# Keys of the recurrent levels written by ScalarE as exponentials of sums, in place of a product on GpSimd

## The reference

```python
def forget(z, lb):
    f = lbh + (1.0 - lbh) * jax.nn.sigmoid(z)
    return 1.0 - f, jnp.log(f)          # key, log of the forget gate
...
cum = jnp.cumsum(lc, axis=2)
rel = cum[:, :, :, None, :] - cum[:, :, None, :, :]
decay = jnp.exp(jnp.where(lower_tri, rel, -jnp.inf))
scores = jnp.einsum('bhtk,bhtsk,bhsk->bhts', qc, decay, kc)
```

## Time and profile before

| | |
|---|---|
| median of 3 runs | 1273.4 us (1273.05 to 1275.78) |
| profiled execution | 1273.12 us |
| its span, first to last instruction | 1271.3 us |
| TensorE busy | 1239.5 us, 98% |
| VectorE busy | 861.2 us, 68% |
| ScalarE busy | 656.2 us, 52% |
| GpSimd busy | 97.3 us, 8% |
| mean granted TensorE clock | 0.996 |

### The profile page before, as it was taken

One profiled execution on the slowest core, in us unless ns is written; L12 is line 12 of the kernel. 1 busy time (PEld: TensorE's weight loads), 2 busy tenths in 40 slices (PEclk: granted clock), 3 DMA queues, 4 the chain that ended last, 5 costly groups with the idle time before them and its releaser, 6 DMA issues.

```text
span 1271.3 us, 22052 instructions
## 1 busy us (share of the span) xinstructions
PE 1239.5 (98%) x9208; PEld 1157.3 (91%) x9208; DVE 861.2 (68%) x1186; ACT 656.2 (52%) x1057; POOL 97.3 (8%) x152
## 2 busy tenths in 40 slices
PE   8999999999999999999999999999999999999998
PEld 7988989988888989989999998889899999999987
DVE  6897677654466677898666554657578987655543
ACT  5896665543368454452544443556563433544432
POOL 2100100000000000550100000000003520000000
PEclk9999999999998999999999999999999999999999
DMA  9542535555525323433555555433343325455552
GB/s 371 211 166 103 197 133 199 195 193 188 188 104 194 127 106 133 140 127 105 197 197 199 190 204 187 167 148 133 103 164 132 134 100 180 157 197 196 199 199 99
DMA packets 30323, 211.77 MB, mean 167 GB/s; under 512 B 3344, under 2 KB 3728, under 8 KB 5264
## 3 DMA queue, kind: packets, MB, share of 16 engines
q1 hardware_dynamic: 29936, 210.22, 46.1%
q10 hardware_dynamic: 288, 0.14, 0.0%
HBM read 209.29 MB, written 1.05 MB: 165 GB/s over the span
## 4 chain that ended last, share of the span: by engine, by line
PE 76%; DVE 12%; ACT 6%; issue 5%; DMA 0%; DVEq 0%; ACTq 0%
PE bank L534 74%; DVE w_lo L1651 3%; ACT w_hi L1152 2%; ACT W L1152 2%; DVE W L1632 1%; PE bank L634 1%; PE bank L869 1%; DVE W L1619 1%; DVE W L1618 1%; DVE xs L2154 1%; DVE W L2132 1%; DVE junk L2152 1%; DVE W L1642 1%; DVE x_lo L1662 0%; DVE stat L1591 0%
## 5 line engine op out<-in xcount | busy, mean ns | idle before, releaser
L1651 DVE TENSOR_TENSOR w_lo<-ring,w_hi 128x2048 fp32r<-128x2048 f32 x183 | 422.2, 2307 | 270.2 <-ACT w_hi L1152 269.8
L1152 ACT ACTIVATE w_hi<-ring 128x1024 fp32r<-128x1024 f32 (+1 forms) x368 | 366.3, 1047 | 223.1 <-PE bank L534 215.2
L534 PE MATMUL bank<-x_hi,w_lo 128*128 128x256 f32 x1840 | 253.8, 277 | 8.6 <-DVE w_lo L1651 7.6
L534 PE MATMUL bank<-x_hi,w_hi 128*128 128x256 f32 x1840 | 259.9, 280 | 2.2 <-ACT w_hi L1152 2.2
L534 PE MATMUL bank<-x_lo,w_hi 128*128 128x256 f32 x1840 | 246.9, 276 | 0.0
L534 PEld LDWEIGHTS bank<-x_hi,w_lo 128*128 128x128 f32 x1840 | 229.2, 188 | 11.4 <-DVE w_lo L1651 10.0
L534 PEld LDWEIGHTS bank<-x_hi,w_hi 128*128 128x128 f32 x1840 | 230.6, 188 | 5.8 <-issue 2.0
L534 PEld LDWEIGHTS bank<-x_lo,w_hi 128*128 128x128 f32 x1840 | 226.5, 188 | 0.0
L534 PE MATMUL bank<-W 128*128 128x128 f32 (+4 forms) x716 | 111.7, 329 | 8.5 <-ACT W L1152 4.8
L534 PEld LDWEIGHTS bank<-W 128*128 128x128 f32 (+3 forms) x716 | 88.0, 188 | 21.6 <-issue 12.5
L534 PE MATMUL bank<-w_hi,hid_hi 128*128 128x512 f32 x304 | 76.6, 389 | 0.0
(11 more groups left out here) (255 smaller groups left out, 1217.3 us busy)
## 6 DMA issues: line engine op xcount, KB each, us to landing
ring<-weight_pieces SPq DMA_DIRECT2D x191, 1024.0 KB, 4.8
const<-constants SPq DMA_DIRECT2D x1, 1376.5 KB, 10.1
W<-x_features SPq DMA_DIRECT2D x4, 256.0 KB, 5.2
ring<-weight_pieces SPq DMA_DIRECT2D x2, 512.0 KB, 6.1
h<-x SPq DMA_DIRECT2D x2, 512.0 KB, 11.9
W<-rg_weights SPq DMA_DIRECT2D x1, 1024.0 KB, 10.5
xs<-mem_features SPq DMA_DIRECT2D x1, 1024.0 KB, 11.3
oT<-mem SPq DMA_DIRECT2D x1, 1024.0 KB, 12.5
```

What stands on the lines that cost most here:

```text
L534: return nc.tensor.matmul(out, lhsT, rhs, start=first, stop=last)
L1152: return nc.scalar.activation(out, in_, ACT.Copy, scale=scale)
L1651: v.tensor_tensor(whole(w_lo, q), rows, whole(w_hi, q).bitcast(F32), ALU.subtract).then_inc(s_weight_low, 1)
```

## The change

The keys' logarithm is taken once in each layer. A new step `keyfloor`, placed in VectorE's list alone, writes the keys with a floor under them into `A_LK`; ScalarE takes their `Ln` right behind that of `F`. After the last scan VectorE makes two versions of the shifted sums: `F`, which now has the logarithm added in the backward half, and `FK`, with the logarithm subtracted in the forward half; that is 4 instructions instead of 2. `level_decay` reads `FK` for its first half, so that the key halves of `A_X` hold the logarithm of decay times key. ScalarE then takes four exponentials of 64x256 for each level and pair: two in place for the queries' decays, and two from `A_X` into `A_KL` for the keys. GpSimd only clears `A_KL`.

```diff
+A_LK = A_GATE + 3072
+A_FK = A_X + 2048
@@ the list of steps
-b[0], ("high", c[0][-1]), ("forget", l, 1), ("low", c[0][-1]), ("high", c[1][-1]), b[1], ...
+b[0], ("high", c[0][-1]), ("forget", l, 1), ("low", c[0][-1]), dve(("keyfloor", l)), ("high", c[1][-1]), b[1], ...
@@ gpsimd, decay
-                    if hp == 0:
-                        if idx:
-                            pool.wait_ge(s_key, idx)
-                        for both_hp in range(2):
...
-                            link(nc.gpsimd.memset(at(A_KL + 512 * ((idx + both_hp) % 4), 2 * S), 0.0))
...
-                    link(nc.gpsimd.tensor_tensor(kl[0:64, :, 0, :], kk[0:64, :, 0, :], x[0:64, :, 0, :], ALU.mult))
-                    nc.gpsimd.tensor_tensor(kl[64:128, :, 1, :], kk[64:128, :, 1, :], x[64:128, :, 1, :], ALU.mult).then_inc(s_key, 1)
+                    if idx >= 4:
+                        prev = idx - 4
+                        wait_filled(pool, f"level{prev // (2 * len(LEVELS))}.{prev // 2 % len(LEVELS)}{prev % 2}")
+                    nc.gpsimd.memset(at(A_KL + 512 * (idx % 4), 2 * S), 0.0).then_inc(s_cleared, 1)
@@ scalar, forget
+                        act.wait_ge(s_key_floor, l + 1)
+                        nc.scalar.activation(at(A_LK, 4 * S), at(A_LK, 4 * S), ACT.Ln).then_inc(s_log_k, 1)
@@ scalar, decay
-                    x = at(A_X + 512 * (idx % 4), 512)
-                    nc.scalar.activation(x, x, ACT.Exp).then_inc(s_decay, 1)
+                    x, kl = (at(a + 512 * (idx % 4), 2 * S).rearrange("p (b w c) -> p b w c", w=2, c=LEVELS[i]) for a in (A_X, A_KL))
+                    nc.scalar.activation(x[0:64, :, 1, :], x[0:64, :, 1, :], ACT.Exp)
+                    nc.scalar.activation(x[64:128, :, 0, :], x[64:128, :, 0, :], ACT.Exp).then_inc(s_decay, 1)
+                    act.wait_ge(s_cleared, idx + 1)
+                    nc.scalar.activation(kl[0:64, :, 0, :], x[0:64, :, 0, :], ACT.Exp)
+                    nc.scalar.activation(kl[64:128, :, 1, :], x[64:128, :, 1, :], ACT.Exp).then_inc(s_key, 1)
@@ vector, level_decay
-                v.tensor_tensor(x[:, :, :, 0, :], mid, f5[:, :, :, 0, :], ALU.subtract)
+                v.tensor_tensor(x[:, :, :, 0, :], mid, fk[:, :, :, 0, :], ALU.subtract)
@@ vector, keyfloor
+                    dve.wait_ge(s_hgrn_k, l + 1)
+                    v.tensor_scalar(at(A_LK, 4 * S), at(A_KK, 4 * S), 2.0 ** -63, None, ALU.max).then_inc(s_key_floor, 1)
@@ vector, after the last scan
+                        dve.wait_ge(s_log_k, l + 1)
                         v.tensor_copy(F[0:64, :, :], E[0:64, :, 1:S + 1])
-                        link(v.tensor_copy(F[64:128, :, :], E[64:128, :, 0:S]))
+                        v.tensor_tensor(F[64:128, :, :], E[64:128, :, 0:S], LK[64:128, :, :], ALU.add)
+                        v.tensor_tensor(FK[0:64, :, :], E[0:64, :, 1:S + 1], LK[0:64, :, :], ALU.subtract)
+                        link(v.tensor_copy(FK[64:128, :, :], E[64:128, :, 0:S]))
```

More of the change, by code:

```diff
@@ L138 @@
 A_KR = 0
+A_LK = A_GATE + 3072
+A_FK = A_X + 2048
 ARENA = A_QKT + 2048
-assert A_X + 2048 <= ARENA and A_SC1 + 6 * 512 <= ARENA
+assert A_FK + 1024 <= ARENA and A_SC1 + 6 * 512 <= ARENA
 def attention_plan():
@@ L276, in build @@
         s_bound_in, s_bound_exp, s_bounds, s_f, s_log_f, s_hgrn_k = (sem(n) for n in ("lb_in", "lb_exp", "lb_ready", "f_ready", "log_f_ready", "hgrn_k_ready"))
+        s_key_floor, s_log_k, s_cleared = sem("key_floor"), sem("log_key_ready"), sem("level_keys_cleared")
         s_decay_log, s_decay, s_query, s_key = (sem(n) for n in ("decay_log", "decay", "level_queries", "level_keys"))
@@ L429, in build @@
             steps += [kr, ("high", b[0][-1]), ("lora", l), ("low", b[0][-1]), ("znorm", l, 0), f1, ("high", b[1][-1]), ("low", b[1][-1]), ("forget", l, 0), ("znorm", l, 1)]
-            steps += [b[0], ("high", c[0][-1]), ("forget", l, 1), ("low", c[0][-1]), ("high", c[1][-1]), b[1], ("zturn", l), ("bsquare", l), c[0], ("low", c[1][-1])]
+            steps += [b[0], ("high", c[0][-1]), ("forget", l, 1), ("low", c[0][-1]), dve(("keyfloor", l)), ("high", c[1][-1]), b[1], ("zturn", l), ("bsquare", l), c[0], ("low", c[1][-1])]
             attend([(f"mla{l}", n) for n in range(4)] + [(f"diff{l}", n) for n in range(4)],
@@ L1615, in level_decay @@
                 x = at(A_X + 512 * (idx % 4), 2 * S).rearrange("p (g b w c) -> p g b w c", g=2, w=2, c=half)
-                f5 = F[:, 2 * hp:2 * hp + 2, :].rearrange("p g (b w c) -> p g b w c", w=2, c=half)
+                fk, f5 = (f[:, 2 * hp:2 * hp + 2, :].rearrange("p g (b w c) -> p g b w c", w=2, c=half) for f in (at(A_FK, 4, S), F))
                 mid = E[:, 2 * hp:2 * hp + 2, half:S:2 * half][:, :, :, None].broadcast_to([P, 2, nb, half])
-                v.tensor_tensor(x[:, :, :, 0, :], mid, f5[:, :, :, 0, :], ALU.subtract)
+                v.tensor_tensor(x[:, :, :, 0, :], mid, fk[:, :, :, 0, :], ALU.subtract)
                 v.tensor_tensor(x[:, :, :, 1, :], f5[:, :, :, 1, :], mid, ALU.subtract).then_inc(s_decay_log, 1)
@@ L1939, in _ @@
                     v.tensor_scalar(F, F, 2.0 ** -63, None, ALU.max).then_inc(s_f, 1)
+                elif kind == "keyfloor":
+                    l = step[1]
+                    dve.wait_ge(s_hgrn_k, l + 1)
+                    v.tensor_scalar(at(A_LK, 4 * S), at(A_KK, 4 * S), 2.0 ** -63, None, ALU.max).then_inc(s_key_floor, 1)
                 elif kind == "bnorm":
@@ L1962, in _ @@
                     if hd == 3:
+                        FK, LK = at(A_FK, 4, S), at(A_LK, 4, S)
+                        dve.wait_ge(s_log_k, l + 1)
                         v.tensor_copy(F[0:64, :, :], E[0:64, :, 1:S + 1])
-                        link(v.tensor_copy(F[64:128, :, :], E[64:128, :, 0:S]))
+                        v.tensor_tensor(F[64:128, :, :], E[64:128, :, 0:S], LK[64:128, :, :], ALU.add)
+                        v.tensor_tensor(FK[0:64, :, :], E[0:64, :, 1:S + 1], LK[0:64, :, :], ALU.subtract)
+                        link(v.tensor_copy(FK[64:128, :, :], E[64:128, :, 0:S]))
                 elif kind == "znorm":
```

9 lines of the change are left out of this document (removed).

## The result

The changed kernel takes 1291.8 us (median of 4 runs, 1291.1 to 1294.1). The kernel before took 1273.5 beside it (4 runs, 1273.05 to 1275.8). The ratio is 1.0146, with a 95% interval from 1.0133 to 1.0158. So it is slower by 18.3 us. The prediction had the sign right and the size wrong by a factor of three, with the time above the end of its range: +5.9 us expected, 1279.3, range to 1287.0. The profiled execution of the changed kernel has a span of 1290.0 us, against 1271.3 before.

The account below looks back on a forecast made before the run. VectorE was taken to bound turns 2 to 5, ScalarE's path turns 0 and 1. Turns with relief +0.95, second `Ln` +0.96 and sums +1.19 make 3.10 us a layer, 6.2 in both: 1279.3 us, range 1274.5 to 1287.

Parts of the forecast that it names:

- The new cycle: Turns, first decay to the next turn's: 8.19 us after the change, 9.14 with the copies in turns 0 and 1.
- The step that failed: Turns, ScalarE: eight 64x256 exponentials priced by a 128x256 row at 0.32 us each, 2.56 us in all.
- The upper bound: Turns: if exponentials do not overlap, eight take 3.36 us, each turn 0.80 more, +9.6 us.
- This rival: Turns: exponentials do not overlap or are slower at narrow strides, 1288.9 us; chance 0.15, shared with blocking clears.
- clears that block VectorE: Turns: GpSimd's clears block VectorE as multiplications do, turns above 9 us, up to 1292 us; chance 0.15, shared.
- the estimate of 2.45 us for eight: Turns: exponentials priced from the Trainium skill at 0.306 us each, giving a total 1.3 us below the forecast.
- The relief ahead of turn 0: VectorE ahead of turn 0: a sum no longer runs beside a GpSimd multiplication, -0.53 us a layer.
- The `Ln`: Second `Ln` on ScalarE, ahead of `w_hi` and four copies TensorE waits for: +0.96 us a layer.
- The sums: Behind the last scan: two added 64x1024 VectorE instructions, 2.30 us, delay `w_lo` and TensorE: +1.19 us a layer.
- the three signs of being wrong: Profile after: eight exponentials at 3 us or more, turns at 7.5, or TensorE's busy time changing beyond the clock term.
- TensorE does not become the limit: Turns: TensorE's own work, taken as 7.5 us a turn, stays below the new cycle.
- The faster rival: Turns: exponentials leave the cycle and TensorE sets the turn at 7.5 us, 1267.3 us; chance 0.05.

Follow-up runs that it names:

- the control with the moved `w_hi`: The kernel before with `w_hi` issued ahead of the decays in turns 0 to 5: 1271.47 us, ratio 0.9971.
- The run on all partitions: The changed kernel with each of its four exponentials over 128 partitions instead of 64, keys first: 1279.98 us, ratio 1.0062.
- one reordered step: The changed kernel with `w_hi` issued ahead of the decays in turns 0 to 5: 1269.22 us, ratio 0.9956.
- two smaller moves: Changed kernel with `w_hi` first, second `Ln` behind the head sums' square, two sums behind the gate drain after the last scan: 1263.0 us, ratio 0.991.

## Why the prediction was wrong

**The bound.** That turns 2 to 5 were bound by VectorE and turns 0 and 1 by ScalarE's path was right. The kernel with GpSimd's multiplications left out and the control with the moved `w_hi` show it from both sides.

**The new cycle.** Right in its parts and in its order: 0.78, `w_hi` 2.04, `w_lo` 2.21, drain 0.60 as taken, and VectorE's wait ahead of `w_lo`, released by ScalarE, at 2.20 to 2.27 us in turns 2 to 5 (1.5 to 2.5 foreseen; 3.3 in turns 0 and 1). The run on all partitions has the predicted cycle to 0.1 us (8.09 for 8.19).

**The step that failed** is "The nearest row is one of 128x256, which lasts 0.42 us and lets the next start after 0.32". The duration held (0.42). The overlap of 0.10 did not, because each exponential of the change works on the other half than the one before it. The term was 2.56 us and measured 3.49 (3.67 in turns 4 and 5, where the narrow halves add 0.18), so 0.93 to 1.11 more a turn. Over 12 turns that is 8 x 0.93 + 4 x 1.11 = 11.9 us of the 12.5 by which the median missed. The upper bound was named, "each costs its whole 0.42, 3.36 in all", and even it was 0.13 short: 0.02 lie between an exponential's end and the next one's start. This rival shared a chance of 0.15 with clears that block VectorE, and its time was 1288.9. The blocking clears' "up to 1292" is nearer in number, but they didn't come: `w_lo` took 2.29 us. The range went only two thirds of the way to 1288.9.

**A row that was there to be read.** The argument against that rival was that `w_hi` overlaps the activations ahead of it. All those run over all 128 partitions. The timeline of before has a pair of ScalarE in a row on opposite halves, copies from the lower to the upper half and back:

```profile
432.39 1.27 ACT L1152 ACTIVATE W<-W 64x512 f32<-64x512 f32 x2 [3.66 <-DVE W L1858]
433.57 0.57 ACT L1152 ACTIVATE xs<-bank 128x512 f32<-128x512 f32 x1
```

Two instructions of 64x512 take 1.27 us, 0.63 each, so they don't overlap. The copy behind them, on all partitions, then overlaps the second, which reads the upper half and writes the lower, by 0.09. So it seems to be the partitions written that count. The copies were not looked for because they aren't exponentials.

**The Trainium skill.** "ScalarE: Activation LUTs", "What ACT_TABLE_LOAD costs", says that back-to-back activations overlap by about 93 ns. The trace agrees where the first partition stays the same (0.40 to 0.42 long, step 0.31 to 0.33) and not for changing halves (step 0.43 to 0.44). The measurement decides, and the estimate of 2.45 us for eight was 1.04 too low.

**The remaining terms.** The relief ahead of turn 0 was right (-0.57 for -0.53), as was that clears don't disturb VectorE: in these turns they run beside its idle time, and in the run without multiplications `w_lo` takes 2.29 us with both clears (2 x 0.52) inside it. `keyfloor` (0.69 us at 400.34) delayed nothing. The `Ln` cost its 0.95 at its place, and half of that was given back in the first layer, where the low-clock stretch turned out shorter. The sums cost 1.41 for 1.19. Copies to `w_hi` took 1.11 instead of 0.95 in turns 0 and 1, 0.6 us in all. They take 0.95 in the run on all partitions, so it goes with the half-partition exponentials ahead of them; how is open. Two queries span 1.5 us instead of 1.28, since the second waits for ScalarE; each lasts 0.69, and nothing hangs on it. Two of the three signs of being wrong came true, the eight at over 3 us and TensorE's busy time, 6.7 us up, which is stretched by its waits.

**"TensorE does not become the limit"** held, and its limit, put at 7.5, is 7.3. The faster rival asked for cheaper exponentials. The way to that side was to take `w_hi` out of the cycle, and the prediction didn't see that the cycle holds only by the order of issue on ScalarE.

## What to carry to other kernels

When an engine is relieved, write down the next cycle instruction by instruction and ask of each whether data or only the order of issue puts it there. Here one reordered step was worth some 22 us on the changed kernel and 3.5 on the one before, and the change that lost 18 gained 11 to 12 with it and two smaller moves. When one instruction is split into several, price them by rows that match in what differs between neighbours (the first partition), not only in size. And TensorE's busy time in a stretch in which it waits is no measure of its own work; a run in which it never waits is.

## What the runs showed of the hardware

- Two activations of ScalarE in a row overlap by about 0.1 us, when nothing holds the second up, if what they write begins at the same partition: both on the lower half, both on the upper, both on all 128, or one on all and one on the lower half. The steps are 0.31 to 0.33 at 0.40 to 0.42 each. They don't overlap at all if one begins at partition 0 and the other at 64 (steps of 0.41 to 0.44). The same eight took 3.49 us alternating, 2.96 in pairs and 2.48 on all partitions.
- In the last two levels, with halves of 2 and 1 tokens, an activation of 256 elements a partition lasts 0.42 to 0.45 us instead of 0.40 to 0.42.
- An activation of 64x256 lasts as long as one of 128x256: 0.40 to 0.42 us. Half the partitions save nothing.
- Without GpSimd's multiplications a turn of 8.0 to 8.6 us fell to the 7.3 of TensorE's own work; two queries took 1.28 us instead of 2.18 and `w_lo` 2.29 instead of 2.82.
- TensorE's busy time for the same products is 7.3 us where it never waits, 7.47 with one wait in a turn of 8.0 and 8.08 with several in a turn of 9.12.
- A stretch at half clock behind an idle time of TensorE comes at different places in the kernels run here, and an idle time of 2.5 us was followed by one before the change and not with the logarithm moved. Executions also differ by 1 to 3 us in parts that no edit touched.
